# Two fp32 transformer blocks on one core: the first mixer's linear-attention steps are placed in other attention units, and x is normed by half blocks

## The chip, the cores and the metric

The kernel runs on one core of a Trainium2 chip. The metric is the device time in microseconds (us), the median of several runs. A profiled execution is one more run, recorded by the hardware profiler. TensorE is called PE here (PEld its weight loads), VectorE DVE, ScalarE ACT, GpSimd POOL, and SyncE SP, which here only issues transfers. Each engine works through its own list of instructions in order; semaphores hold an instruction until what it needs is there.

## The reference

Two blocks follow each other on x of 512 tokens by 1024 channels, all in fp32. Only the first mixer is touched by the change:

```python
u = rmsnorm(x, norm_mix_pre)
proj = u @ w_in        # qa ka va ga za | qs ks vs
# gated linear attention, 4 heads, chunks of 64 tokens, forwards and backwards
la = log_sigmoid(z @ w_gate_up + b_gate) / 16      # z: 16 of the 32 za columns
b = cumsum(la within a chunk)
q_dec, k_intra, k_state = q * exp(b), k * exp(-b), k * exp(b_last - b)
# windowed attention, 8 heads of 64, blocks of 128 tokens, keys of the block and its neighbours
logits = q @ k.T * 0.125 + rel_bias                # plus one sink logit per head
p = softmax(logits); o_s = p @ v
h = x + rmsnorm(concat(o_a, o_s) @ w_out)          # then an MLP, then the second block
```

## The kernel before

A product in fp32 quality is made of three products of rounded halves: a value is split in an upper part (rounded, made by ACT with a copy: `w_hi`, `act_hi`) and a lower part (value minus upper, made by DVE: `w_lo`, `act_lo`). `mm3` on PE multiplies hi by hi, hi by lo and lo by hi (L805 to L807).

The first mixer reads w_in in chunks c = 0 to 9 of 256 columns through two slots (`raw`, `w_hi`, `w_lo`). SP loads a chunk into its slot of `raw` when the lower part of the chunk two before has been made (`lo_done`). Chunks 0 and 1 are the queries of the windowed attention, 2 its keys and values, 3 the columns za (`zz`, only 128 columns are multiplied), 4 and 5 `qa` and `ka`, 6 and 7 `va_tok`, 8 and 9 `ga`.

**Start.** PE spreads the gain of the norm over the partitions (L836, into `psT`, two banks). ACT takes each block's sum of squares and its root (`first_scale`, L1442 to L1447), DVE multiplies the block of 128 tokens of x with its scale and the gain (`first_normed`, L2100, into `un`), PE turns it (`turn_first`, L858), ACT writes the upper part (`first_turned`, L1460) and DVE the lower part (L2109). Chunks 0 and 1 (`project_queries`) are multiplied for token blocks 0 and 1 as soon as those are turned (half 0, four groups of 24 matmuls named by a half of K and a slot: (0,0), (0,1), (1,0), (1,1)); blocks 2 and 3 are turned in between, and half 1 follows.

**The order of the rest** is one list of steps (`mixer1_steps`), which every engine walks and of which it takes its share. After chunks 2 and 3 come 18 attention units k = 0 to 17 (`attention_unit(k, work)`). Unit k holds, in this order: the logits matmuls of attention step k (`qk`, L1071), the transposes of the probabilities of step k-1 (`transpose`, PE L1082; ACT then copies them to `pT`, L1564), the softmax of step k (DVE L1964 to L1971, then ACT's two exponentials, L1556), at every fourth unit a `spread` of the inverse sums by DVE (L1983), then `work`, then at every fourth unit `turn` (PE L1106, ACT copy L1568, and DVE's product L1994 at the end of the unit), and the product with the values of step k-1 (`pv`, L1096). `work` is half an output tile of a chunk (12 matmuls of 512 columns, or 24 of 256 for the values), ACT's upper part of the next chunk (`split_hi`, L1435) at k = 0, 4, 8, 12, 16, DVE's lower part (`split_lo`, L1808) at k = 1, 5, 9, 13, 17, and the steps of the linear attention. These come four times, i = 0 to 3 (direction i % 2, channel half i // 2):

- `gla_gate`: PE L1114 multiplies the gate, DVE L2002 adds the bias, ACT does three functions (L1575 to L1577);
- `gla_decay`: DVE does three operations, the running sum among them (L2008, L2014, L2020), ACT three exponentials (L1583, L1584, L1586);
- `gla_scaled`: POOL makes two scaled key tiles (L1351, L1353, L1356; two SBUF inputs each), DVE copies the decay and scales the query (L2027, L2031);
- `gla_keys`: PE turns one of the key tiles (L1120), ACT copies it (L1589).

In the kernel before, gate, decay and scaled of i stand at the end of units 4 to 15, three units for each i (gate of i = 0 in front of the work of unit 4), so that decay 0 and 3 and scaled 1 fall into units with a lower part; keys stand in units 8, 11, 14 and 17.

**Between chunks 2 and 3** the step `keys_values` does three things: ACT copies the keys to the other 64 partitions (L1546, L1547), PE turns the values v (L1057), and ACT copies those out (L1549). `split` of chunk 4 and the tile of chunk 3 follow it.

Of the kernel before, what the change touches and what calls it, by code (L numbers as in the profile page):

```python
# [8 lines left out]
ALU = mybir.AluOpType  # L9
# [5 lines left out]
NBLK = TOK // P  # L15
# [186 lines left out]
def block_kernel(nc, a, out):  # L202
    ctx = ExitStack()
    with ctx:
# [338 lines left out]

        def mixer1_steps():
            steps = first_steps(0)
            steps += [("keys_values", 0), ("split", 4), ("tile", 3, 1)]
            k = 0
            for c in (4, 5, 6, 7, 8):
                for m, half in enumerate(half_tiles(c)[:2 if c == 8 else 4]):
                    work = [half]  # L550
                    if m == 0 and c < 9:
                        work.insert(0, ("split_hi", c + 1))
                    if m == 1 and c < 9:
                        work.insert(0, ("split_lo", c + 1))
                    if k >= 8 and k % 3 == 2:
                        work.insert(0, ("gla_keys", (k - 8) // 3))
                    if 4 <= k <= 15:
                        gla = (("gla_gate", "gla_decay", "gla_scaled")[(k - 4) % 3], (k - 4) // 3)
                        work.insert(0 if k == 4 else len(work), gla)
                    steps += attention_unit(k, work)  # L560
                    k += 1
            rest = half_tiles(8)[2:] + half_tiles(9)
            steps += [("gla_dS", 0), rest[0], rest[1], ("wsplit", N_O0, 1), ("gla_dS", 1), rest[2], rest[3],
                      ("gla_A", 0), rest[4], ("gla_A", 1), rest[5], ("attention_halves", 0),
                      ("gla_out", 0), ("gla_out", 1), ("gla_sum", 0), ("gla_sum", 1)]
            return steps
# [235 lines left out]
        def _(pe):  # L802
# [9 lines left out]
            def project_queries():  # L812

                for half in range(2):
                    cols = slice(HALF * half, HALF * half + HALF)
                    pe.wait_ge(act_lo_done, 4 * half + 4)
                    for kh, s in ((0, 0), (0, 1), (1, 0), (1, 1)) if half == 0 else ((0, 0), (1, 0), (0, 1), (1, 1)):
                        if half == 0:
                            pe.wait_ge(lo_done if kh else first_lo, s + 1)
                        for j in range(2):  # L820
                            for k in range(4 * kh, 4 * kh + 4):
                                last = mm3(acc[:, 2 * s + j, cols], *w_tiles(s, k, j),
                                           act_hi[:, k, cols], act_lo[:, k, cols], k == 0, k == KT - 1)
                            if half and kh:
                                last.then_inc(tile_done[j], 1)
                        if half == 0 and (kh, s) == (0, 0):
                            turn_tables()
                        if half == 0 and (kh, s) == (0, 1):
                            turn_first(2)
                    if half == 0:  # L830
                        turn_first(3)

            pe.wait_ge(const_in, 16)
            pe.wait_ge(gain1_in, 16)
            for g in range(2):
                last = pe.matmul(psT[:, g, :], ones[0:1, :], gain_row[:, 512 * g:512 * g + 512], start=True, stop=True)  # L836
            last.then_inc(gain1_ps, 1)

            def turn_tables():

# [6 lines left out]

            def turn_first(b):

                pe.wait_ge(un1_done, b + 1)  # L850
                if b >= 2:
                    pe.wait_ge(act_lo_done, 2 * (b - (1 if b == 3 else 2)) + 2)
                    if b == 2:
                        pe.wait_ge(vec_done, 1)
                        pe.wait_ge(relf_sb, 1)
                for g in range(2):
                    for k in range(4):
                        last = pe.transpose(first_bank(b, g)[:, k * P:(k + 1) * P],  # L858
                                            un1[:, b, (4 * g + k) * P:(4 * g + k + 1) * P], ident[:, :])
# [179 lines left out]
            def mixer_step_pe(layer, step, at):  # L1039
# [8 lines left out]
                elif what == "pair":  # L1048
                    project_queries()
                    last_in_bank.update({0: 0, 1: 1})  # L1050
                elif what == "keys_values":
                    if layer == 0:
                        pe.wait_ge(evac_done, 6)
                    else:
# [353 lines left out]
        def _(act):  # L1408
# [107 lines left out]
            def boundary_blocks(s, following):  # L1516
# [14 lines left out]
                    hi(N_AB, 0)  # L1531
                hi_turned(s, NBLK - 1)

            def mixer_step_act(layer, step):
                what, i = step[0], step[1]
                k = 16 * layer + i
# [1 line left out]
                    split(i)  # L1538
                elif what in ("wsplit", "upper"):
                    hi(i, step[2])  # L1540
                elif what == "keys_values":
                    if layer == 0:
                        act.wait_ge(evac_done, 6)
                    else:
                        act.wait_ge(evD_done, evacs_before(TILE_AT[N_KV, 0], "D") + 1)
                    act.activation(KX[layer][64:128, :], KH[layer][0:64, :], ACT.Copy).then_inc(kx_done, 1)  # L1546
                    act.activation(KX[layer][0:64, :], KH[layer][64:128, :], ACT.Copy).then_inc(kx_done, 1)  # L1547
                    act.wait_ge(vT_done, layer + 1)
                    act.activation(VTOK[layer][:, :, :], ps7[:, :].rearrange("p (b n) -> p b n", b=NBLK), ACT.Copy)\  # L1549
                       .then_inc(vtok_done, 1)  # L1550
                elif what == "softmax":
                    w = len(window(layer, i // 4)[0]) * P + 1
                    act.wait_ge(negmax_done, k + 1)
# [71 lines left out]
            first_scale(0)  # L1625
            first_scale(1)
            first_upper(0, 0)
            first_upper(0, 1)
            first_turned(0)
            first_turned(1)  # L1630
            first_scale(2)
            first_upper(1, 0)
# [166 lines left out]
        def _(dve):  # L1799
# [295 lines left out]
            def first_normed(b):  # L2095

                dve.wait_ge(rs1_done, b + 1)
                if b == 0:
                    dve.wait_ge(gain1_ps, 1)
                dve.scalar_tensor_tensor(out=un1[:, b, :], in0=x_tok[:, b, :], scalar=st1[:, b, 1:2],  # L2100
                                         in1=psT[:, :, :].rearrange("p g n -> p (g n)"), op0=ALU.mult, op1=ALU.mult)\
                   .then_inc(un1_done, 1)

            def first_lo_turned(b):

# [248 lines left out]
```

## Time and profile before

| | |
|---|---|
| runs | 1011.2, 1007.82, 1011.0 us, median 1011.0 |
| profiled execution | 1009.43 us, of it span 1007.6 us |
| PE busy | 980.5 us (97%) |
| DVE, ACT, POOL busy | 561.1, 397.4, 55.9 us |
| PE busy from 64 to 162 us (attention units) | 90.03 of 98 us |
| first matmul of the first product | at 16.31 us |

Start and duration are in us from the start of the span. A row in brackets says how long the engine had stood idle before the instruction and who ended it. PE is busy nearly throughout; where it stands is what the time could give.

### The profile page before, as it was taken

To read this page: it belongs to the slowest core of one execution; us is meant where nothing else is said; L and a number is where in the kernel's file an instruction comes from. 1 tells how busy PE (TensorE), PEld (TensorE's weight loads), DVE (VectorE), ACT (ScalarE), POOL (GpSimd) and SP (SyncE) were. 2 spreads that over 40 slices of the span, in tenths; PEclk is the share of its full clock that TensorE was granted. 3 is DMA by queue.
4 is the path that set the end of the run, shared out by engine and by line. 5 is a ranking of instruction groups with operands and counts; after the bars stand their busy time and mean duration, and the time that the engine had idled before them with its cause. 6 is when DMAs were issued, how large, how long until landed. Compare 5 with 4: busy or idle time off the path is not lost.

```text
span 1007.6 us, 12804 instructions
## 1 busy us (share of the span) xinstructions
PE 980.5 (97%) x5280; PEld 782.7 (78%) x5280; DVE 561.1 (56%) x721; ACT 397.4 (39%) x646; POOL 55.9 (6%) x49
## 2 busy tenths in 40 slices
PE   6999999999999999999999999999999999999997
PEld 4876777878888888888888888877778877667786
DVE  3356777657541244344234375356755568889953
ACT  5144563276432243134214354434564620222541
POOL 4000112000000000000000000003000100100300
PEclk9999999999999999999999999999999999999999
DMA  6942002232233322233222223422041556556112
GB/s 197 148 137 59 20 24 85 85 126 89 96 121 114 126 84 84 84 108 137 90 83 84 84 84 96 167 84 84 1 155 42 194 164 155 133 150 191 43 73 83
DMA packets 63361, 104.83 MB, mean 104 GB/s; under 512 B 3974, under 2 KB 27399, under 8 KB 63176
## 3 DMA queue, kind: packets, MB, share of 16 engines
q1 hardware_dynamic: 62968, 103.77, 32.9%
q8 instruction: 42, 0.69, 0.3%
q10 hardware_dynamic: 336, 0.25, 0.1%
q14 instruction: 15, 0.12, 0.0%
HBM read 99.43 MB, written 4.58 MB: 103 GB/s over the span
## 4 chain that ended last, share of the span: by engine, by line
PE 85%; DVE 9%; ACT 2%; issue 2%; DMA 1%; SPq 0%; DVEq 0%
PE acc L805 25%; PE acc L806 24%; PE acc L807 24%; PE psT L1082 2%; PE acc L1071 1%; PE psT L971 1%; PE ps L1096 1%; DVE wlr L1848 1%; DVE psT L2241 1%; PE psT L950 1%; DMA raw<-in_w_in_dram 1%; PE ps L971 1%; DVE sm L1970 1%; DVE rt L1875 1%; DVE stat L2256 0%
## 5 line engine op out<-in xcount | busy, mean ns | idle before, releaser
L805 PE MATMUL acc<-act_hi,wh 128*128 128x512 f32 x464 | 183.9, 396 | 0.3 <-DVE wlr L1848 0.3
L1848 DVE TENSOR_TENSOR wlr<-wl,wh 128x2048 fp32r<-128x2048 f32 (+1 forms) x66 | 145.2, 2204 | 64.7 <-ACT wh L1472 64.7
L807 PE MATMUL acc<-act_hi,wlr 128*128 128x512 f32 x464 | 181.1, 390 | 0.0
L806 PE MATMUL acc<-act_lo,wh 128*128 128x512 f32 x464 | 180.9, 390 | 0.0
L1472 ACT ACTIVATE wh<-wl 128x2048 fp32r<-128x2048 f32 (+1 forms) x68 | 124.3, 1832 | 60.0 <-DMA wl<-in_w_up_dram 34.2
L805 PE MATMUL acc<-wh,act_hi 128*128 128x512 f32 (+1 forms) x352 | 133.7, 380 | 0.6 <-DVE act_lo L1892 0.6
L807 PE MATMUL acc<-wh,act_lo 128*128 128x512 f32 (+1 forms) x352 | 130.6, 371 | 0.0
L806 PE MATMUL acc<-wlr,act_hi 128*128 128x512 f32 (+1 forms) x352 | 130.4, 371 | 0.0
L805 PEld LDWEIGHTS acc<-act_hi,wh 128*128 128x128 f32 x464 | 87.2, 188 | 22.9 <-issue 4.2
L807 PEld LDWEIGHTS acc<-act_hi,wlr 128*128 128x128 f32 x464 | 87.1, 188 | 18.6
L806 PE MATMUL acc<-wlr,hid_hi 128*128 128x512 f32 x256 | 100.9, 394 | 0.0
L806 PEld LDWEIGHTS acc<-act_lo,wh 128*128 128x128 f32 x464 | 87.3, 188 | 17.1
L805 PE MATMUL acc<-wh,hid_hi 128*128 128x512 f32 x256 | 100.6, 393 | 0.0
L807 PE MATMUL acc<-wh,hid_lo 128*128 128x512 f32 x256 | 99.5, 389 | 0.0
L805 PEld LDWEIGHTS acc<-wh,act_hi 128*128 128x128 f32 x352 | 66.5, 189 | 13.1 <-issue 1.6
L806 PEld LDWEIGHTS acc<-wlr,act_hi 128*128 128x128 f32 x352 | 66.5, 189 | 11.3 <-issue 0.7
L807 PEld LDWEIGHTS acc<-wh,act_lo 128*128 128x128 f32 x352 | 66.3, 188 | 11.4
L805 PE MATMUL acc<-act_hi,w_hi 128*128 128x512 f32 (+1 forms) x152 | 55.2, 363 | 4.0 <-DVE act_lo L2109 3.7
L1655 ACT ACTIVATE zr<-acc 128x512 f32<-128x512 f32 x32 | 19.2, 599 | 99.7 <-PE acc L807 99.7
L805 PEld LDWEIGHTS acc<-wh,hid_hi 128*128 128x128 f32 x256 | 48.1, 188 | 11.1
L807 PEld LDWEIGHTS acc<-wh,hid_lo 128*128 128x128 f32 x256 | 48.1, 188 | 10.6
L806 PEld LDWEIGHTS acc<-wlr,hid_hi 128*128 128x128 f32 x256 | 48.3, 189 | 9.5
(238 smaller groups left out, 1378.0 us busy)
## 6 DMA issues: line engine op xcount, KB each, us to landing
wl<-in_w_up_dram SPq DMA_DIRECT2D x16, 1024.0 KB, 6.4
wl<-in_w_down_dram SPq DMA_DIRECT2D x16, 1024.0 KB, 6.3
wl<-in_c_w_in_dram SPq DMA_DIRECT2D x20, 512.0 KB, 4.9
raw<-in_w_in_dram SPq DMA_DIRECT2D x18, 512.0 KB, 5.2
shifted<-glu_dram SPq DMA_DIRECT2D x32, 262.0 KB, 4.7
wl<-in_a_w_in_dram SPq DMA_DIRECT2D x8, 1024.0 KB, 6.2
wl<-in_w_out_dram SPq DMA_DIRECT2D x4, 1024.0 KB, 6.3
wl<-in_ab_w_out_dram SPq DMA_DIRECT2D x4, 1024.0 KB, 7.5
```

The source lines that it names most:

```text
L805: pe.matmul(dst, hi, x_hi, start=first, stop=False)
L806: pe.matmul(dst, hi, x_lo, start=False, stop=False)
L807: return pe.matmul(dst, lo, x_hi, start=False, stop=last)
L950: last = pe.transpose(psT[:, g, (k % 4) * P:(k % 4 + 1) * P], un[:, b % 2, k * P:(k + 1) * P], ident[:, :])
L971: last = pe.matmul(xsum(t)[32 * c:32 * c + 32, :], tapw[:, t % 2, 4 * m + c, :], shifted[:, t % 2, c, 4 * m:4 * m + TOK], start=m == 0, st ...
L1071: last = pe.matmul(acc[:, 2 + j, 0:len(kbs) * P], QH[layer][h64, hp, n * P:(n + 1) * P], keys[h64, kbs[0] * P:(kbs[-1] + 1) * P], start=Tr ...
L1082: last = pe.transpose(psTf[:, (2 * b + j) * P:(2 * b + j + 1) * P], LG[layer][:, i % 2, j, 1 + b * P:1 + (b + 1) * P], ident[:, :])
L1096: last = pe.matmul(ps6[64 * j:64 * j + 64, hp * P:(hp + 1) * P], VTOK[layer][:, kb, 64 * g:64 * g + 64], PT[layer][:, (2 * b + j) * P:(2 * ...
L1472: act.activation(wh[slot][:, kk, cols], wl[slot][:, kk, cols], ACT.Copy).then_inc(whi_done, 1)
L1655: act.activation(zr[:, m % 2, :], acc[:, TILES[e][2], :], ACT.Relu).then_inc(zr_done, 1)
L1848: dve.tensor_tensor(wlr[slot][:, kk, cols], wl[slot][:, kk, cols], wh[slot][:, kk, cols].bitcast(F32), ALU.subtract).then_inc(wlo_done, 1)
L1875: dve.scalar_tensor_tensor(out=rt[:, b, :], in0=yg[:, b, :], scalar=ssq[:, s, 12 + b:13 + b], in1=rt[:, b, :], op0=ALU.mult, op1=ALU.add). ...
```

## The change

It has four parts.

1. `first_normed` is done by halves of 512 channels, each after its own half of the spread gain, and `turn_first` waits by halves. On ACT the upper part of block 0 (`first_turned(0)`) comes before the upper part of chunk 1's first half (`first_upper(0, 1)`).
2. `turn_first(3)` stands on PE between the groups (1,0) and (1,1) of half 0, not behind (1,1).
3. `keys_values` is cut in two: `keys` (ACT's two copies) stays; `values` (PE's transposes and ACT's copy) comes behind the tile of chunk 3.
4. Gate, decay, scaled and keys have other units: gates at the end of units 2, 6, 10, 14; decays in front of the work of units 3, 7, 11, 15; scaled in front of that of units 6, 8, 12, 16; keys in front of that of units 7, 10, 14, 17.

```diff
-            steps += [("keys_values", 0), ("split", 4), ("tile", 3, 1)]
+            steps += [("keys", 0), ("split", 4), ("tile", 3, 1), ("values", 0)]
+            gla_first = {3: [("gla_decay", 0)], 6: [("gla_scaled", 0)], 7: [("gla_keys", 0), ("gla_decay", 1)],
+                         8: [("gla_scaled", 1)], 10: [("gla_keys", 1)], 11: [("gla_decay", 2)], 12: [("gla_scaled", 2)],
+                         14: [("gla_keys", 2)], 15: [("gla_decay", 3)], 16: [("gla_scaled", 3)], 17: [("gla_keys", 3)]}
+            gla_last = {2: ("gla_gate", 0), 6: ("gla_gate", 1), 10: ("gla_gate", 2), 14: ("gla_gate", 3)}
...
-                    if k >= 8 and k % 3 == 2:
-                        work.insert(0, ("gla_keys", (k - 8) // 3))
-                    if 4 <= k <= 15:
-                        gla = (("gla_gate", "gla_decay", "gla_scaled")[(k - 4) % 3], (k - 4) // 3)
-                        work.insert(0 if k == 4 else len(work), gla)
+                    work = gla_first.get(k, []) + work
+                    if k in gla_last:
+                        work.append(gla_last[k])
...
-                        if half == 0 and (kh, s) == (0, 1):
-                            turn_first(2)
-                    if half == 0:
-                        turn_first(3)
+                        if half == 0 and (kh, s) in ((0, 1), (1, 0)):
+                            turn_first(2 + kh)
...
-                last = pe.matmul(psT[:, g, :], ones[0:1, :], gain_row[:, 512 * g:512 * g + 512], start=True, stop=True)
-            last.then_inc(gain1_ps, 1)
+                pe.matmul(psT[:, g, :], ones[0:1, :], gain_row[:, 512 * g:512 * g + 512], start=True, stop=True)\
+                  .then_inc(gain1_ps, 1)
...
-                pe.wait_ge(un1_done, b + 1)
...
+                    pe.wait_ge(un1_done, 2 * b + g + 1)
...
             first_upper(0, 0)
+            first_turned(0)
             first_upper(0, 1)
-            first_turned(0)
             first_turned(1)
...
-                dve.scalar_tensor_tensor(out=un1[:, b, :], in0=x_tok[:, b, :], scalar=st1[:, b, 1:2],
-                                         in1=psT[:, :, :].rearrange("p g n -> p (g n)"), op0=ALU.mult, op1=ALU.mult)\
-                   .then_inc(un1_done, 1)
+                for g in range(2):
+                    if b == 0:
+                        dve.wait_ge(gain1_ps, g + 1)
+                    cols = slice(512 * g, 512 * g + 512)
+                    dve.scalar_tensor_tensor(out=un1[:, b, cols], in0=x_tok[:, b, cols], scalar=st1[:, b, 1:2],
+                                             in1=psT[:, g, :], op0=ALU.mult, op1=ALU.mult).then_inc(un1_done, 1)
```

ACT around the keys and values of the windowed attention: the rows begin with chunk 3's upper part and end with the first softmax. Before:

```order
L1433 ACTIVATE w_hi<-raw 128x8x128
L1546 ACTIVATE k1x<-k_72 64x512
L1547 ACTIVATE k1x<-k_72 64x512
L1549 ACTIVATE v_tok<-ps 128x512
L1435 ACTIVATE w_hi<-raw 128x2048
L1556 ACTIVATE lg_76,sums_80<-lg_76,sm_78 128x257 x2
```

Now:

```order
L1433 ACTIVATE w_hi<-raw 128x8x128
L1554 ACTIVATE k1x<-k_72 64x512
L1555 ACTIVATE k1x<-k_72 64x512
L1435 ACTIVATE w_hi<-raw 128x2048
L1537 ACTIVATE v_tok<-ps 128x512
L1563 ACTIVATE lg_76,sums_80<-lg_76,sm_78 128x257 x2
```

The upper part of chunk 4 (L1435) has moved in front of the copy of the turned values; on PE the turning itself stands behind the 24 matmuls of chunk 3's tile instead of in front of them.

DVE in units 5 and 6: from the last row of softmax 5 to the scaled query of i = 0 (`sq` is the gate tile here, `sq_sum` the running sum). Before:

```order
L1971 TENSOR_SCALAR sm_78<-sm_78 128x2
L1808 TENSOR_TENSOR w_lo<-raw,w_hi 128x2048
L1818 COPY ka<-acc 128x512
L2008 SCALAR_TENSOR_TENSOR sq<-sq 128x512
L2014 SCALAR_TENSOR_TENSOR sq_sum<-restart,sq 128x512
L2020 TENSOR_TENSOR sq<-sq_sum 128x512
L1964 COPY lg_76<-sink_82 128x2
L1965 SCALAR_TENSOR_TENSOR lg_76<-acc,bias_70 128x2x384
L1970 TENSOR_REDUCE sm_78<-lg_76 128x2
L1971 TENSOR_SCALAR sm_78<-sm_78 128x2
L2027 COPY decay<-eb 128x8
L2031 SCALAR_TENSOR_TENSOR qdec_f<-qa,eb 128x512
```

Now:

```order
L1978 TENSOR_SCALAR sm_78<-sm_78 128x2
L1815 TENSOR_TENSOR w_lo<-raw,w_hi 128x2048
L1825 COPY ka<-acc 128x512
L1971 COPY lg_76<-sink_82 128x2
L1972 SCALAR_TENSOR_TENSOR lg_76<-acc,bias_70 128x2x384
L1977 TENSOR_REDUCE sm_78<-lg_76 128x2
L1978 TENSOR_SCALAR sm_78<-sm_78 128x2
L2034 COPY decay<-eb 128x8
L2038 SCALAR_TENSOR_TENSOR qdec_f<-qa,eb 128x512
L2009 TENSOR_SCALAR sq<-ps,vec 128x512
```

Decay 0 has left the place between the lower part and softmax 6, and gate 1 has come in behind the scaled query.

DVE in units 3 and 4, from softmax 3 on. Before:

```order
L1971 TENSOR_SCALAR sm_78<-sm_78 128x2
L1818 COPY qa<-acc 128x512
L1964 COPY lg_76<-sink_82 128x2
L1965 SCALAR_TENSOR_TENSOR lg_76<-acc,bias_70 128x2x384
L1970 TENSOR_REDUCE sm_78<-lg_76 128x2
L1971 TENSOR_SCALAR sm_78<-sm_78 128x2
L1979 RECIPROCAL rsum_81<-sums_80 128x8
L1983 COPY spread_79<-rsum_81 128x512
L2002 TENSOR_SCALAR sq<-ps,vec 128x512
L1994 TENSOR_TENSOR o_60<-ps,o_60 128x4x128
```

Now:

```order
L1978 TENSOR_SCALAR sm_78<-sm_78 128x2
L2015 SCALAR_TENSOR_TENSOR sq<-sq 128x512
L2021 SCALAR_TENSOR_TENSOR sq_sum<-restart,sq 128x512
L2027 TENSOR_TENSOR sq<-sq_sum 128x512
L1825 COPY qa<-acc 128x512
L1971 COPY lg_76<-sink_82 128x2
L1972 SCALAR_TENSOR_TENSOR lg_76<-acc,bias_70 128x2x384
L1977 TENSOR_REDUCE sm_78<-lg_76 128x2
L1978 TENSOR_SCALAR sm_78<-sm_78 128x2
L1986 RECIPROCAL rsum_81<-sums_80 128x8
L1990 COPY spread_79<-rsum_81 128x512
L2001 TENSOR_TENSOR o_60<-ps,o_60 128x4x128
```

Decay 0 now stands right behind softmax 3, ahead of the copy of `qa` and of softmax 4, and the gate's bias is no longer in unit 4.

## Rows read from the trace of the kernel before

**Rows 1.** The page's chain that ended last: shares of the span by engine

```profile
PE 85%; DVE 9%; ACT 2%; issue 2%; DMA 1%; SPq 0%; DVEq 0%
```

**Rows 2.** What PE waited for, 0 to 260 us: total, times, longest

```profile
PE psT L1082 <- ACT lg L1556: 4.1, 4, 1.4
PE acc L805 <- DVE act_lo L2109: 3.7, 2, 2.2
PE ps L1096 <- ACT pT L1564: 2.1, 1, 2.1
...
PE ps L1106 <- DVE spread L1983: 1.4, 1, 1.4
PE ps L1057 <- DVE v L1818: 0.8, 1, 0.8
```

**Rows 3.** Two stretches: PE, PEld, DVE, ACT, POOL busy; clock, DMA share, GB/s

```profile
64.00:162.00 98.00, 90.03 (x640) 68.38 (x638) 68.23 (x116) 55.78 (x116) 10.14 (x8) 1.00 0.15 44
...
205.00:586.00 381.00, 381.00 (x1696) 314.14 (x1695) 164.39 (x160) 137.44 (x178) 0.00 (x0) 1.00 0.28 100
```

**Rows 4.** Timeline of PE at the start: start, duration, instruction

```profile
5.25 3.75 PE L836 MATMUL psT<-gain_row,ident_ones 1*128 1x512 f32 x4 [5.25 <-DMA gain_row<-in_norm_mix_pre_dram]
...
16.31 0.58 PE L805 MATMUL acc<-act_hi,w_hi 128*128 128x256 f32 x1 [2.18 <-DVE act_lo L2109]
...
19.68 0.36 PE L805 MATMUL acc<-act_hi,w_hi 128*128 128x256 f32 x1
...
20.83 0.25 PE L843 MATMUL ps<-ident_ones,vec_rows 97*128 97x97 f32 x1
...
34.16 0.39 PE L805 MATMUL acc<-act_hi,w_hi 128*128 128x256 f32 x1 [1.57 <-DVE act_lo L2109]
```

**Rows 5.** Timelines of ACT and DVE at the start

```profile
12.20 1.06 ACT L1453 ACTIVATE w_hi<-raw 128x1024 fp32r<-128x1024 f32 x1 [1.39 <-DMA raw<-in_w_in_dram]
...
14.12 1.08 ACT L1460 ACTIVATE act_hi<-acc 128x512 fp32r<-128x512 f32 x2
...
9.12 2.47 DVE L2100 SCALAR_TENSOR_TENSOR un<-x_tok,st,psT 128x1024 f32<-128x1024 f32 x2 [9.12 <-PE psT L836]
...
14.97 1.28 DVE L2109 TENSOR_TENSOR act_lo<-acc,act_hi 128x512 fp32r<-128x512 f32 x2
```

**Rows 6.** Timelines of PE and ACT around chunks 3 and 4

```profile
64.65 0.47 PE L805 MATMUL acc<-act_hi,w_hi 128*128 128x512 f32 x1 [0.23 <-DVE zz L1818]
...
50.56 1.06 ACT L1433 ACTIVATE w_hi<-raw 128x1024 fp32r<-128x1024 f32 x1 [8.36 <-DMA raw<-in_w_in_dram]
...
59.40 1.92 ACT L1435 ACTIVATE w_hi<-raw 128x2048 fp32r<-128x2048 f32 x1
```

**Rows 7.** Timelines of PE, DVE and POOL in units 5 and 6

```profile
88.56 0.88 PE L1082 MATMUL psT<-ident_ones,lg 128*128 128x128 f32 x6
92.14 0.88 PE L1096 MATMUL ps<-pT,v_tok 128*64 128x128 f32 x12
...
99.96 0.88 PE L1096 MATMUL ps<-pT,v_tok 128*64 128x128 f32 x12 [2.06 <-ACT pT L1564]
...
95.56 0.68 DVE L2008 SCALAR_TENSOR_TENSOR sq<-sq 128x512 f32<-128x512 f32 x1
...
98.15 0.16 DVE L1964 COPY lg<-sink 128x2 f32<-128x2 f32 x1
...
100.20 1.19 DVE L1971 TENSOR_SCALAR sm<-sm 128x2 f32<-128x2 f32 x1
...
100.08 1.28 POOL L1353 TENSOR_TENSOR sq_sum<-ka,sq 128x512 f32<-128x512 f32 x1
```

**Rows 8.** Groups of 64 to 162 us by shape: busy us, mean ns

```profile
L1808 DVE TENSOR_TENSOR w_lo<-raw,w_hi 128x2048 fp32r<-128x2048 f32 x4 | 9.1, 2284 | 0.0
...
L1965 DVE SCALAR_TENSOR_TENSOR lg<-acc,bias 128x768 f32<-128x768 f32 x8 | 7.6, 950 | 0.0
...
L1556 ACT ACTIVATE lg<-lg,sm 128x385 f32<-128x385 f32 x16 | 9.7, 609 | 10.4 <-DVE sm L1971 10.4
```

More of the change, by code:

```diff
@@ L1050, in mixer_step_pe @@
                     last_in_bank.update({0: 0, 1: 1})
-                elif what == "keys_values":
+                elif what in ("keys_values", "values"):
                     if layer == 0:
@@ L1532, in boundary_blocks, with values_turned @@
                 hi_turned(s, NBLK - 1)
+            def values_turned(layer):
+                act.wait_ge(vT_done, layer + 1)
+                act.activation(VTOK[layer][:, :, :], ps7[:, :].rearrange("p (b n) -> p b n", b=NBLK), ACT.Copy)\
+                   .then_inc(vtok_done, 1)
             def mixer_step_act(layer, step):
@@ L1540, in mixer_step_act @@
                     hi(i, step[2])
-                elif what == "keys_values":
+                elif what == "values":
+                    values_turned(layer)
+                elif what in ("keys_values", "keys"):
                     if layer == 0:
@@ L1547, in mixer_step_act @@
                     act.activation(KX[layer][0:64, :], KH[layer][64:128, :], ACT.Copy).then_inc(kx_done, 1)
-                    act.wait_ge(vT_done, layer + 1)
-                    act.activation(VTOK[layer][:, :, :], ps7[:, :].rearrange("p (b n) -> p b n", b=NBLK), ACT.Copy)\
-                       .then_inc(vtok_done, 1)
+                    if what == "keys_values":
+                        values_turned(layer)
                 elif what == "softmax":
@@ L2097, in first_normed @@
                 dve.wait_ge(rs1_done, b + 1)
-                if b == 0:
-                    dve.wait_ge(gain1_ps, 1)
-                dve.scalar_tensor_tensor(out=un1[:, b, :], in0=x_tok[:, b, :], scalar=st1[:, b, 1:2],
-                                         in1=psT[:, :, :].rearrange("p g n -> p (g n)"), op0=ALU.mult, op1=ALU.mult)\
-                   .then_inc(un1_done, 1)
+                for g in range(2):
[4 more added lines that the diff above has]
+                                             in1=psT[:, g, :], op0=ALU.mult, op1=ALU.mult).then_inc(un1_done, 1)
             def first_lo_turned(b):
```

## Prediction

> **What bounds the kernel now.** I read the chain that ended last first: PE holds 85% of it, and ACT, DVE and transfers together 12% [rows 1]. So a microsecond counts only where PE stands. Next I read PE's own waits of the first 260 us, the part that the change touches [rows 2]. From the first product to the end of the attention units PE stands 12.1 us: 3.7 us in two waits for lower parts of x, 0.8 us for the values v, and in the units 4.1 us in four waits for ACT's exponentials, 2.1 us in one wait for the copy `pT`, 1.4 us for `spread`. The units' three entries are 7.6 us; the stretch from 64 to 162 us agrees (98 less 90.03 busy, with some issue time) [rows 3]. From 205 to 586 us PE is never idle and its loads are released by its own tiles, so what is won before is kept, and no more than these 12 us is to be had [rows 3].
>
> **Part 1, half blocks.** The first matmul of the product starts at 16.31, when DVE has ended the lower part of block 1 (14.97 + 1.28) [rows 4, 5]. Before it ACT worked off the upper part of chunk 1 at 12.20, which waits for its transfer, then block 0's two copies, and block 1's from 14.12 [rows 5]. Now block 0's copies (1.0 us) go into the 1.39 us in which ACT stood before 12.20. For that block 0 must be turned by about 11: the first half of the gain's four passes (5.25 to 9.0) [rows 4] is done near 7.2, DVE's first half block (0.65, a quarter of 2.47) near 7.9, its second follows the gain's end 9.0 and is done at 9.75 [rows 5]. PE turns from 9.0 on without the wait that it had, and ends block 0 near 11. The transfer sets 12.20 as before, so block 1's copies start at about 13.2, DVE's last lower part ends near 15.05, and PE starts at 15.1: 1.2 us. Below that nothing is gained beyond 0.7 if the copies of block 0 don't fit; above it the clock decides, see the rivals.
>
> **Part 2, block 3.** PE turns block 3, then stands 1.57 us before 34.16 for copy and lower part [rows 4]. With 24 matmuls of group (1,1) behind the turning (24 at the later pace: 9 in 1.15 us, so 3.1 us) the copy and the lower part, 1.57 + about 1 us of turning overlap, are hidden. Gain 1.55.
>
> **Part 3, keys and values.** PE no longer waits 0.8 us for v [rows 2]. Let T be the end of chunk 2's tiles (56.9 before). Before, chunk 4's tile starts at 64.65, T + 7.8 [rows 6]. Now PE needs T + 6.7 (tile 5.4, turning 0.6, logits 0.7), while ACT's key copies end at T + 2.0, the upper part of chunk 4 (1.92) at T + 3.95, DVE's lower part (2.28) at T + 6.25 [rows 6, 8] and the copy of `zz` behind it at T + 6.9. Chunk 4's tile waits for both: T + 7.0, gain 0.8, with 0.3 us of the wait moved to `zz`. The price if the cover is gone: chunk 3 lands at 50.5 [rows 6] and comes now after T only if T falls under 53; its upper part, lower part and the copy of k end at about 53.5 where nothing moves its transfer, and T becomes 56.9 less 2.75, or 54.1. That is 0.6 us of margin, and the transfer itself is released by DVE's table copy, which comes earlier too. So nothing is added.
>
> **Part 4, the units.** Why PE stands now: in unit 5 DVE does softmax 5, the lower part (2.28), `ka`, then decay 0 (95.56 to 98.15, 2.6 us) before softmax 6 [rows 7, 8]. ACT's three decay exponentials wait for the sum and stand in front of the copy `pT`, so pv waits 2.06 us at 99.96, and softmax 6 is late for the next transposes [rows 7]. Decay 3 repeats it in unit 14, scaled 1 in unit 9, and decay 2 in unit 11 delays the spread.
>
> Now I lay the units end to end by these durations: logits 0.85 (0.63 with two key blocks), transposes and pv 0.81 or 0.59, half a tile 2.75 (from 88.56 + 0.81 to 92.14) [rows 7], values 2.95, DVE's softmax 2.15 (two of 0.95 and two small ones), ACT's pair of exponentials 1.2 (two of 0.609) [rows 8], decay 2.6. A loop from logits to transposes must fit into one unit. The tightest places come out so:
> - Unit 6, transposes of step 5. From the end of pv 3: ACT ends the upper part of chunk 6 at +0.8, the `turn` copy at +1.3; DVE's product at +1.9, softmax 5 at +4.1; exponentials +5.3. PE: logits 0.85, transposes 0.81, half a tile 2.75, pv 0.81, logits 0.85, in all 6.1. Margin 0.8.
> - Unit 12, spread behind decay 2 and softmax 12: 0.4 of margin.
> - Steps 9, 13 and 15: 1.2 to 1.6, two of them with a lower part but no decay in front of them, or the decay behind the softmax.
> - pv behind the decay's three exponentials: 1.5 or more, since these now start early in the unit.
>
> No decay shares a unit with a lower part, and nothing waits twice. The 7.6 us go to near 0; for the misses of such a sum I leave 0.4.
>
> What speaks against it is POOL. At 100.20 DVE's negation (1.19 us, else 0.17) lies over POOL's key product of 100.08 to 101.36 and ends with it [rows 7]: 1.0 us lost. The scaled keys now start with the softmax of their unit, in units 6, 8 and 12, so the sink's copy or the negation will be held again. By my laying out it is 0.4 us in unit 6, up to 1.3 in unit 8, 1.0 in unit 12, and all of it inside the margins of 1.3, 2.6 and 2.0 of those transposes; but unit 8's may push the spread 0.35 past PE.
> The Trainium skill (SBUF — State Buffer, "SBUF: two separate sides") calls the port pair of DVE and GpSimd an exclusive lock that is held for a whole instruction, while the loser fully blocks. By that rule, the trace agrees: the stall ends with POOL's instruction, and eight products could hold DVE for up to 1.3 us each; the sum would change by the 0.35 us alone.
>
> **Sum.** 1.2 + 1.55 + 0.8 + 7.6 - 0.4 = 10.75 us. The profiled execution took 1009.4 with a span of 1007.6; less 10.75 it is 998.7. It lies 1.6 us under the median 1011.0 of the runs, within their spread of 3.4. I say 999.2. The bound from above is the 12 us of all waits plus 1.5 of clock, from below the sure parts.
>
> **Rivals.**
> - *The units keep half of their waits* (each softmax late by a held negation or a queue that I laid too tight): 3.8 us stay, 1003. Speaks for it: margins of 0.4 and 0.8 us are small. Against: waits that are missed so add tenths. Chance 0.17.
> - *The waits only move*: the 2.6 us of DVE's decay in front of `qa`, `ka` and softmax 4, 8, 12 take the place of those removed, and only parts 1 to 3 count: 1009.4 - 3.55 = 1005.9, 1007 by the median. DVE's busy 68 of 98 us speaks against it [rows 3]. Chance 0.08.
> - *The clock.* The first 15 matmuls take 3.37 us, 0.225 each (the half level, 1.2 GHz), those from 19.68 to 20.83 take 0.128 (2.4 GHz) [rows 4]. Before them PE had stood 2.18 us. PE now works from 5.25 to about 13 with no gap, so the rise may come before the product: 15 times 0.1, 1.5 us more, 997.7. Or the rise stays at 19.7 and half of part 1 is lost, 0.6. Chance of the early rise 0.1.
>  The Trainium skill (TensorE: Matmul & The Clock Gate, "What's actually happening") says that the default state is throttled and activity releases the throttle; by it the first matmuls would gain as in this rival.
> - *Slower.* One mechanism: the loop through DVE and ACT, not PE, is the bound of the units. Then each of the four decays costs its 2.6 us and each of the four pairs of key products 2.5: 20.4 in all against the 11.1 us won, so 1018. It decides from the point where the units have no margin; the loop of unit 6 above would have to be 0.8 us longer and all others 1.2 to 2.6. The two engines stand 30 and 42 of 98 us [rows 3], most of it within each unit. Chance 0.03.
>
> **Numbers.** Forecast 0.62 (997 to 1001), the others 0.17, 0.08, 0.10, 0.03. The likeliest time is 999.2; the range for 8 in 10 takes in the early clock and half of the units' waits: 996.5 to 1003.5. A measurement of this kernel tells some 0.5% (5 us) from no change. Faster by more than that: 0.62 + 0.17 + 0.10, less 0.02 for a stay near the edge, 0.87; within it 0.10; slower 0.03.
>
> **What would show it.** The first matmul of the product near 15.1, the restart of half 1 near 31.4 with no wait, chunk 4's tile near 61, pv 15 ended near 151 instead of 162; in PE's waits no entry over 0.5 us for exponentials, `pT` or spread. DVE's small copies or negations of about 1.2 us beside POOL in units 6, 8 and 12 without a wait of PE behind them. I am wrong if PE waits for exponentials in units 6, 8, 9 or 12, if chunk 3 comes after T, or if a stretch behind 205 us has a wait that it did not have.

## The result and the profile after

The changed kernel takes 997.93 us (median of 4 runs, 996.52 to 998.65); the kernel before, run beside it, 1009.88 (4 runs, 1007.82 to 1011.2). The ratio is 0.9882 with a 95% interval of 0.9858 to 0.9906: faster by 1.2%. 999.2 was forecast. The profiled execution took 998.65 us (span 996.9), against 1009.43 (span 1007.6) before: 10.7 us less of span. It was the slowest of the four runs of after; the other three have no trace.

PE's waits from 0 to 250 us, as in [rows 2]: total, times, longest.

```profile
PE psT L836 <- DMA ident_ones<-in_shapes_dram: 5.4, 1, 5.4
PE acc L807 <- DVE act_lo L2117: 1.7, 1, 1.7
PE ps L1114 <- ACT o L1596: 0.8, 1, 0.8
PE acc L807 <- DVE zz L1825: 0.5, 1, 0.5
```

The entries for exponentials (4.1), `pT` (2.1), `spread` (1.4) and the values (0.8) are gone, and one of two waits for a lower part. New are 0.8 us of the gate's matmuls; the wait for `zz` has grown from 0.2 to 0.5. A wait of 1.5 us for the normed block, ahead of block 0's turning, is gone too. The two stretches of [rows 3], moved to where the same work now lies:

```profile
60.00:151.00 91.00, 89.66 (x644) 68.64 (x641) 67.02 (x117) 56.69 (x117) 10.28 (x8) 1.00 0.15 47
...
194.00:575.00 381.00, 381.00 (x1695) 313.85 (x1695) 164.56 (x160) 137.62 (x178) 0.00 (x0) 1.00 0.28 100
```

PE stands 1.3 us where it stood 8, with nearly the same matmuls (644 and 640 rows); 381 us of the later stretch are as full as before, so what is won ahead of it stays won. PE at the start and at chunk 4 (start, duration, instruction), for [rows 4] and [rows 6]; the row at 21.40 is the second group of the product:

```profile
9.10 2.03 PE L858 MATMUL ps<-ident_ones,un 128*128 128x128 f32 x8
...
14.57 0.58 PE L807 MATMUL acc<-act_hi,w_hi 128*128 128x256 f32 x1 [1.74 <-DVE act_lo L2117]
...
19.64 0.41 PE L809 MATMUL acc<-act_hi,w_lo 128*128 128x256 f32 x1
19.86 0.36 PE L843 MATMUL ps<-ident_ones,vec_rows 97*128 97x97 f32 x1
20.15 1.32 PE L846 MATMUL ps<-hot,relw 33*8 33x512 f32 x2
21.40 0.39 PE L807 MATMUL acc<-act_hi,w_hi 128*128 128x256 f32 x1
...
61.50 0.47 PE L807 MATMUL acc<-act_hi,w_hi 128*128 128x512 f32 x1 [0.54 <-DVE zz L1825]
```

The same second group in the kernel before:

```profile
21.01 1.02 PE L846 MATMUL ps<-hot,relw 33*8 33x512 f32 x2
21.96 0.39 PE L805 MATMUL acc<-act_hi,w_hi 128*128 128x256 f32 x1
```

The product starts 1.74 us earlier, but all 24 matmuls of its first group now run at the half level (0.213 us apart), where 15 did before, and so do part of the small table matmuls behind them (L843, L846). The next group starts only 0.56 us earlier: the clock takes 1.18 us, 0.77 in the group and 0.41 in the tables. Half 1 starts near 31.9 with no wait, and chunk 4's tile 3.15 us earlier. The rows of pv 15 end at 151.24 (150.58 and 0.66) and before at 162.11 (161.45 and 0.66): 10.87 us earlier, so 7.72 come from the units.

ACT at the start, for [rows 5]: block 0's two copies lie ahead of chunk 1's upper part (L1453), as laid out. The second one is the first row here. The upper part follows it without a gap, though its transfer had landed near 11.4 (issued at 2.1, 9.3 us to landing): in this execution the copies held it by 0.25 us.

```profile
11.16 0.60 ACT L1460 ACTIVATE act_hi<-ps 128x512 fp32r<-128x512 f32 x1 [0.32 <-PE ps L858]
11.65 1.05 ACT L1453 ACTIVATE w_hi<-raw 128x1024 fp32r<-128x1024 f32 x1
12.60 1.08 ACT L1460 ACTIVATE act_hi<-acc 128x512 fp32r<-128x512 f32 x2
```

DVE, POOL and PE in units 6, 8 and 12, for [rows 7]:

```profile
93.66 0.69 DVE L1978 TENSOR_SCALAR sm<-sm 128x2 f32<-128x2 f32 x1
...
104.50 0.94 DVE L1978 TENSOR_SCALAR sm<-sm 128x2 f32<-128x2 f32 x1
...
105.58 0.43 DVE L1990 COPY spread<-rsum 128x512 f32<-128x512 f32 x1
...
128.35 1.31 DVE L1990 COPY spread<-rsum 128x512 f32<-128x512 f32 x1
...
93.03 1.29 POOL L1353 TENSOR_TENSOR sq_sum<-ka,sq 128x512 f32<-128x512 f32 x1
...
104.12 1.30 POOL L1356 TENSOR_TENSOR ka<-ka,sq 128x512 f32<-128x512 f32 x1
...
128.08 1.29 POOL L1353 TENSOR_TENSOR sq_sum<-ka,sq 128x512 f32<-128x512 f32 x1
...
106.07 0.65 PE L1106 MATMUL ps<-ident_ones,spread 128*128 128x128 f32 x4
...
129.99 0.60 PE L1106 MATMUL ps<-ident_ones,spread 128*128 128x128 f32 x4
```

Three small operations of DVE (0.17, 0.17 and 0.43 us where POOL rests) take 0.69, 0.94 and 1.31. The first two end within 0.03 us of the end of a key product of POOL, the third 0.29 us behind it. No wait of PE stands behind them: `spread` is done at 106.01 and 129.66, the turning that needs it starts at 106.07 and 129.99.

### The profile page after: what moved, and what is told of

Read it like the earlier page. It is cut to its first block, busy times and chain, and to the rows that moved or that the text cites. A ratio compares the mean times of both kernels' runs of the same rounds, so it can differ in the third digit from the quotient of the medians.

```text
span 996.9 us, 12808 instructions
## 1 busy us (share of the span) xinstructions
PE 980.5 (98%) x5280; PEld 782.9 (79%) x5280; DVE 559.6 (56%) x725; ACT 398.0 (40%) x646; POOL 56.3 (6%) x49
## 4 chain that ended last, share of the span: by engine, by line
PE 88%; DVE 8%; ACT 2%; issue 2%; DMA 0%; DVEq 0%
PE acc L807 25%; PE acc L808 25%; PE acc L809 25%; PE acc L1071 2%; PE ps L1096 2%; PE psT L1082 2%; PE psT L971 1%; DVE wlr L1855 1%; DVE psT L2249 1%; PE psT L950 1%; PE ps L971 1%; DVE rt L1882 1%; DVE stat L2264 1%; DVE ysum L2239 0%; DMA ident_ones<-in_shapes_dram 0%
## 5 line engine op out<-in xcount | busy, mean ns | idle before, releaser
L808 PEld LDWEIGHTS acc<-wlr,act_hi 128*128 128x128 f32 x352 | 66.4, 189 | 11.4 <-issue 0.7
L809 PEld LDWEIGHTS acc<-wh,hid_lo 128*128 128x128 f32 x256 | 48.1, 188 | 10.7
```

Source lines behind the costliest of these rows:

```text
L808: pe.matmul(dst, hi, x_lo, start=False, stop=False)
L809: return pe.matmul(dst, lo, x_hi, start=False, stop=last)
```

## Experiments

Times are medians; "the kernel before" was run beside each (medians 1009.0, 1008.9, 1009.1 in the three groups of runs). "After without" undoes one part. After itself was measured beside a median of 1009.9 for the kernel before, so its time and that of an experiment come from different groups: medians alone do not tell differences of under 1 us between the two. Where such a difference counts, the steadier measure is a stretch of the trace, as from the start of the product's second group to chunk 4's tile: 42.66 to 42.70 us in all five kernels that have neither part 2 nor part 3.

**Part 4 alone** (`units_only`) and **after without part 4** (`no_units`):

```diff
# the kernel before with:
+            gla_first = {3: [("gla_decay", 0)], 6: [("gla_scaled", 0)], ...}
+            gla_last = {2: ("gla_gate", 0), ...}
-                    if k >= 8 and k % 3 == 2: ...
-                    if 4 <= k <= 15: ...
+                    work = gla_first.get(k, []) + work
+                    if k in gla_last:
+                        work.append(gla_last[k])
```

> The kernel before with part 4 alone: gate, decay, scaled and keys in the new units. My theory (the waits of the units came from a decay or a scaled step in a unit that also has a lower part, and they are gone): the start and chunk 4's tile stand where they stood (16.3 and 64.65), pv 15 ends near 154.3 instead of 162.04, PE's waits in the units fall from 7.6 us to under 1, in all 7.7 us faster, a ratio near 0.9924. Rival (the parts need each other, the earlier start makes the room in the units): under 5 us faster. Rival (waits were paid by the clock or by chance between executions): pv 15 moves by less than 3 us.

Measured: 1000.91 us (999.48 to 1001.16), ratio 0.9917 (0.9902 to 0.9933).

> The changed kernel with part 4 undone (parts 1 to 3 alone). Theory: parts 1 to 3 are worth 3.15 us (chunk 4's tile at 61.5 instead of 64.65) and the units keep their 7.6 us of waits: ratio near 0.997 against the kernel before, pv 15 ended near 159. Rival (the earlier start lets the units' waits shrink too): more than 5 us faster.

Measured: 1005.85 us (1004.1 to 1007.45), 0.9966 (0.9953 to 0.998); all waits of the units are back (4.1, 2.1, 1.4). Part 4 is worth 8.1 us alone and 7.9 with the rest by the medians, 7.8 and 7.7 by the stretch from chunk 4's tile to pv 15: the parts add, and it is most of the gain.

**Part 1 alone** (`start_only`, half blocks and ACT's swap) and **after without part 1** (`no_start`); the edits are part 1's lines of the diff above.

> The kernel before with part 1 alone: x by half blocks and ACT's swap. Theory: the first matmul of the product comes at 14.6 instead of 16.3; if the clock rises as late as in the changed kernel (only after 20 us), the second group of matmuls starts 0.5 us earlier only and the whole gain is 0.5 us, ratio 0.9995; if it rises 3.4 us behind the first matmul as in the kernel before, the gain is 1.7 us. The wait of 1.57 us in front of half 1 stays in both cases, since block 3 is still turned behind all of half 0.

> The changed kernel with part 1 undone (parts 2 to 4). Theory: first product matmul at 16.1 to 16.3, all else kept: 0.6 to 1.8 us slower than the changed kernel (by how late the clock rises in it), about 999.5. Rival (parts 2 or 4 need the earlier start, as the turning of block 3 then comes before its block is normed): over 2.5 us slower, with a wait of PE before the transposes of block 3.

Measured: 1007.73 (1005.91 to 1008.74), 0.9985 (0.9975 to 0.9995); and 998.83 (996.75 to 999.37), 0.9892 (0.9876 to 0.9909), 0.9 more than after. Some 1 us, at the limit of what the runs tell. The traces are sharper. The transfer of chunk 1 lands at a time that differs from one execution to the next: with the old order ACT starts its upper part at the landing, at 11.15 (`turn3_only`) to 12.20 us (before). From the upper part's start to the first matmul of the product it is 4.11 to 4.12 us in every kernel with the old order (before 12.20 to 16.31; `units_only` 11.76 to 15.88; `no_start` 12.02 to 16.14) and 2.91 to 2.92 in every kernel with part 1 (after 11.65 to 14.57; `start_only` 11.63 to 14.55). Where ACT has its copies done before the landing, as in `start_only`, part 1 gives these 1.20 us. In after it had not, and 0.25 of them are lost: the old order would have put the product at 11.4 + 4.12 = 15.5, so some 1.0 of the 1.74 us is part 1, and some 0.75 is a transfer that happened to come earlier.

In `start_only` the first group has 15 slow matmuls, as before, and the second group starts 1.83 us earlier, with nothing lost to the clock; the wait ahead of half 1 stays (1.57). In `no_start` the stretch from the second group to chunk 4's tile is that of after (40.11 and 40.10 us): parts 2 and 3 do not need part 1.

**ACT's swap alone** (`swap_only`, in the kernel before):

```diff
             first_upper(0, 0)
+            first_turned(0)
             first_upper(0, 1)
-            first_turned(0)
```

> The kernel before with only ACT's order changed: block 0's two copies ahead of the upper part of chunk 1's first half; the norm stays in whole blocks. Theory of the prediction (the swap needs the half blocks, since block 0 must be turned by about 11): block 0 is turned at 12.4, ACT's two copies end near 13.0, the upper part of chunk 1 near 14.0, block 1's copies near 15.1 against 15.2 before, and the product starts at 16.1 to 16.3, nothing won (1008.8 to 1009). Rival: the swap alone wins what part 1 wins, the first matmul at 15.1 or earlier.

Measured: 1008.0 (1007.06 to 1010.24), 0.9986 (0.9975 to 0.9996).

```profile
9.06 1.06 ACT L1453 ACTIVATE w_hi<-raw 128x1024 fp32r<-128x1024 f32 x1 [0.88 <-DMA raw<-in_w_in_dram]
11.25 0.60 ACT L1460 ACTIVATE act_hi<-ps 128x512 fp32r<-128x512 f32 x1 [1.13 <-PE ps L858]
12.11 0.60 ACT L1460 ACTIVATE act_hi<-ps 128x512 fp32r<-128x512 f32 x1 [0.26 <-PE ps L858]
12.60 1.05 ACT L1453 ACTIVATE w_hi<-raw 128x1024 fp32r<-128x1024 f32 x1
...
15.51 0.38 PE L805 MATMUL acc<-act_hi,w_hi 128*128 128x256 f32 x1 [1.73 <-DVE act_lo L2109]
```

The second upper part of w starts at 12.60 behind the late copies. Its data was there near 11.5 (issued at 2.1, 9.4 us to landing), and the old order would have put the product at 15.6. The swap alone wins some 0.1 us; it needs the half blocks. The profiled execution (1007.06 us) is faster for two other causes: its transfer came 0.7 us earlier than that of before, and its 24 first matmuls are all 0.12 us apart (below). What makes up the 1 us of the medians is not shown; the other nine runs have no trace.

**Part 2 alone** (`turn3_only`, in the kernel before; the edit is part 2's lines of the diff):

> The kernel before with part 2 alone: block 3 is turned between the groups (1,0) and (1,1) of half 0. Theory: it pays by itself, as copy and lower part are hidden under 3.1 us of matmuls: no wait ahead of half 1, whose first matmul comes at 32.5 instead of 34.16, chunk 4's tile at 63.0, time 1007.3 (1.6 to 1.75 less). Rival: it pays only behind part 1, since with the later start DVE's first block sets when blocks 2 and 3 are normed and the turning of block 3 now waits in the middle of the half; then a wait of 1 us or more stands ahead of the turning of block 3 and the time is 1008.5 or more.

Measured: 1006.26 (1005.65 to 1009.28), 0.9973 (0.9961 to 0.9985). Half 1 starts at 31.53 without a wait. From the start of the second group, where the clock is at its full level in both, to chunk 4's tile it is 40.86 us against 42.69: part 2 gives 1.83 us by itself. The median is 2.8 us under that of before; what the rest is, the trace of one execution does not show.

**Decay 0 back at the end of unit 5** (`decay0_back`, in after):

```diff
-            gla_first = {3: [("gla_decay", 0)], 6: ...
+            gla_first = {6: ...
+                    if k == 5:
+                        work.append(("gla_decay", 0))
```

> The changed kernel with decay 0 alone moved from the front of unit 3 to the end of unit 5, which has a lower part (where it stood before). Theory (the collision in one unit is the cause): DVE does softmax 5, lower part, ka, decay 0 and only then softmax 6; pv 4 or the transposes of step 6 wait again, 2 to 3.5 us in all in units 5 to 7, nowhere else, 1000.5 in all. Rival (what counts is DVE's total or the gate's place): under 0.5 us of new wait.

Measured: 999.61 (999.08 to 1000.2), 0.9907 (0.9888 to 0.9926), 1.7 more than after. PE in units 6 and 7:

```profile
94.55 0.88 PE L1098 MATMUL ps<-pT,v_tok 128*64 128x128 f32 x12 [0.90 <-ACT pT L1573]
...
97.36 0.88 PE L1084 MATMUL psT<-ident_ones,lg 128*128 128x128 f32 x6 [1.09 <-ACT lg L1565]
```

One decay behind a lower part brings back both kinds of wait of [rows 7], the copy `pT` behind ACT's exponentials and the transposes behind a late softmax: 2.0 us for one misplaced step (the stretch to pv 15 is 2.07 us longer).

**The two waits that the change brought** (`better`, in after): keys 1 one unit earlier, chunk 4's upper part ahead of the copies of the keys.

```diff
-            steps += [("keys", 0), ("split", 4), ("tile", 3, 1), ("values", 0)]
+            steps += [("split", 4), ("keys", 0), ("tile", 3, 1), ("values", 0)]
-                         8: [("gla_scaled", 1)], 10: [("gla_keys", 1)], ...
+                         8: [("gla_scaled", 1)], 9: [("gla_keys", 1)], ...
```

> The changed kernel with two steps moved: keys 1 from unit 10 to unit 9, and the upper part of chunk 4 in front of the two key copies on ACT. Theory: the wait of 0.8 us before gate 2 in unit 10 was for ACT's copy of keys 1, which stands behind the exponentials of its own unit, and the 0.54 us before chunk 4's tile was for zz, whose copy stands on DVE behind the lower part of chunk 4: both go, 1.3 us faster than the changed kernel, about 996.6. Rival (another wait stands right behind each, as the transposes of step 9): under 0.5 us.

Measured: 996.99 (995.92 to 997.67), 0.9877 (0.9862 to 0.9891), 0.9 less than after, which the medians alone would not tell. The stretches do: from the second group to chunk 4's tile 39.51 us against 40.10, and from that tile to pv 15 0.55 us less, 1.1 in all of the 1.3 expected. All of PE's waits up to 250 us are now:

```profile
PE psT L836 <- DMA ident_ones<-in_shapes_dram: 5.0, 1, 5.0
PE acc L807 <- DVE act_lo L2117: 2.3, 1, 2.3
PE ps L1120 <- issue: 0.3, 1, 0.3
```

In after, the cause of the 0.8 us was this row of ACT, with the softmax of its unit ahead of it:

```profile
117.89 0.57 ACT L1596 ACTIVATE o<-ps 128x512 f32<-128x512 f32 x1
...
118.61 1.09 PE L1114 MATMUL ps<-zz,gate_w 32*128 32x512 f32 x2 [0.81 <-ACT o L1596]
```

In unit 10 the turned keys are copied out behind the two exponentials of step 10, and gate 2 needs the same PSUM bank at the end of the unit. In unit 9 the copy has a unit's time.

**Unused matmuls in PE's gap.** `fill_gap` is after with four matmuls of the identity, whose product nobody reads, behind the turning of block 1; `warm_early` has these and eight more ahead of the gain, on a tile that POOL clears first; `fill_before` has the four in the kernel before.

```diff
             turn_first(0)
             turn_first(1)
+            for _ in range(4):
+                pe.matmul(acc[:, 0, 0:P], ident[:, :], ident[:, :], start=True, stop=True)
```

> The changed kernel with work for PE that no result uses: 8 small matmuls on a zeroed tile before the gain and its constants have landed, and 4 behind the turning of block 1, where PE stands 1.7 to 2.1 us. If the clock follows PE's activity, PE reaches the high level before or soon after 5 us, the gain and the turning take half their time, and the 24 matmuls of the first group run at 0.12 us instead of 0.22: the first product matmul still comes near 14.4 (ACT and the transfer set it), its group ends 2.4 us sooner, tile of chunk 4 near 59.1, 2.4 us faster than the slowest start seen (chunk 4's tile at 61.5), 1 us than the fastest (60.07). Rival (the rise is a matter of chance in each execution, whatever PE does): slow matmuls at the start as before.

> The changed kernel with the 4 extra matmuls in the gap between the turning of block 1 and the product alone. Theory: PE is then busy without a gap from 5.3 us on and the rise comes before 17 us; the first group has under 12 slow matmuls. Rival (the start of PE's work, not the gap, sets it): 14 to 24 slow ones as in the kernels without it.

> The kernel before with only the four unused matmuls put behind the turning of block 1, where PE stands for 2.18 us. Theory that PE's standing ahead of the product is what has it start at the half level: no slow matmul among the first group, its 24 matmuls take 3 us instead of 4.5 (15 slow ones by 0.1), chunk 4's tile at 63.1 instead of 64.65, the rest unchanged, time 1007.4 (1.5 less). Rival: the clock rises at a fixed time near 19.6 whatever PE does before the product (as the last slow matmul of five of the eight kernels so far would have it): 15 slow matmuls, no change of the time beyond 0.1 us.

Measured: `warm_early` 997.48 (995.55 to 998.0), 0.9879 (0.9863 to 0.9895); `fill_gap` 995.88 (995.75 to 996.19), 0.9867 (0.9851 to 0.9884), 2.0 less than after; `fill_before` 1007.89 (1007.08 to 1010.0), 0.9991 (0.998 to 1.0002), not told from no change by its runs. `warm_early`, which also has the four, is only 0.5 us under after: its profiled run took 995.55 us, the other three 997.4 to 998.0. PE in `fill_gap`, with the four matmuls in the first row:

```profile
12.45 1.81 PE L865 MATMUL acc<-ident_ones 128*128 128x128 f32 x8
14.58 0.39 PE L807 MATMUL acc<-act_hi,w_hi 128*128 128x256 f32 x1 [0.32 <-DVE act_lo L2119]
14.80 0.28 PE L808 MATMUL acc<-act_lo,w_hi 128*128 128x256 f32 x1
14.92 0.28 PE L809 MATMUL acc<-act_hi,w_lo 128*128 128x256 f32 x1
```

The product starts where it did in after (14.57) and runs at the full level. Its second group starts at 18.68 instead of 21.40, 2.7 us earlier, which is the whole loss to the clock in the profiled execution of after (6.83 us from the product's start to the second group, here 4.10). The matmuls ahead of the gain in `warm_early` did nothing: the gain and block 0's turning still took as long. The four do not close the gap: PE still stood 0.32 us behind them in `fill_gap`, 1.24 in `best` and 1.59 in `fill_before`, without a slow matmul, where `turn3_only` stood 1.52 us without them and had 17. So it is what PE did before it stood, or chance, and not the length of the standing alone.

**All three finds together** (`best`: `better` with the four unused matmuls):

> The kernel after with the three edits found good so far together: the keys' step of i = 1 in unit 9, the upper part of chunk 4 ahead of the copies of the keys, and four unused matmuls behind the turning of block 1. If the two unit edits and the filling of PE's gap are independent of each other, their gains add: the product starts at 14.6 with no slow matmul, chunk 4's tile comes near 58.2, the chunk 8 and 9 stretch as in the kernel with the filling less another 1 to 1.4 us, so the end of the third keys' turning is at 147.4 to 147.9 and the time 994.6 to 995.2 us. Rival: the faster start brings a new wait (chunk 3's transfer comes after the tiles of chunk 2), which takes the unit edits' 1.3 us back; then chunk 4's tile is at 58.8 or later and the time is 995.9, that of the filling alone.

Measured: 995.0 us (994.42 to 995.16), 0.9854 (0.9837 to 0.9872). It is the fastest kernel, 2.9 us under after; the gains add (0.9 and 2.0 by the medians). Chunk 4's tile starts at 57.81 with no wait, and the turned keys of i = 3 come at 147.28 (162.36 before).

```profile
PE psT L836 <- DMA ident_ones<-in_shapes_dram: 5.1, 1, 5.1
PE acc L807 <- DVE act_lo L2119: 1.2, 1, 1.2
PE ps L1122 <- issue: 0.3, 1, 0.3
```

## Why the prediction held, by its own steps

**Part 1, forecast 1.2, is 1.20** where the copies of block 0 fit ahead of the transfer, and some 1.0 in after, where they end 0.25 late; the step named this loss (nothing beyond 0.7 if they don't fit) but took the transfer to land at 12.20 as before. And the rival in which the clock stays low till 19.7 took 1.18 us, more than all of part 1, and not the 0.6 that I gave it: 0.77 in the first group, and 0.41 in the tables behind it, which I had left out. By chance the transfer came some 0.75 us earlier and made up for over half of that.

**Part 2, forecast 1.55, is 1.83.** The term held the wait alone. But PE's next instruction overlaps the end of the one before it, and ahead of a wait this overlap is lost too. Block 2's turning, with work ready behind it, is followed after 0.79 us (24.94 to 25.73); block 3's in the kernel before runs to its end, 1.03 us, before the wait begins. That is 0.24 of the 0.26 us beyond the wait of 1.57.

**Part 3, forecast 0.8, is 0.76.** From the second group to chunk 4's tile it is 40.86 us with part 2 alone and 40.10 to 40.12 in all six kernels with parts 2 and 3 and keys first. The wait moved to `zz` as the step said, 0.54 instead of 0.3. In `better`, which makes chunk 4's upper part first, it is gone, worth another 0.6. Chunk 3 did not become late: its upper part starts at 50.66, T is 54.3 (54.1 forecast), and PE does not wait for it.

**Part 4, forecast 7.6 less 0.4 for misses, is 7.72.** No wait for exponentials, `pT` or `spread` is left. The miss was real, and twice as large: 0.8 us at gate 2, where keys 1 (ACT's copy) stands behind the softmax of unit 10. I had laid out DVE's and ACT's loops up to the transposes and pv, but not the gate's matmuls, which need the bank of the turned keys. What made up for it: the six waits of the units held 7.6 us, and the stretch is 7.72 shorter with 0.8 of new wait in it, so 0.9 more went than waits show. Some 0.2 of it has no wait: gate 0 no longer stands between the transposes and the tile of unit 4, where the transposes took 0.59 us to the next start (82.09 to 82.68), now 0.41 (80.01 to 80.42). Some 0.5 is the overlap lost ahead of a wait, as in part 2: 0.06 us where logits stand before it (92.94 to their end 93.85, where an undisturbed unit has 0.85 to the next start), 0.2 in unit 12. The rest I can't place. It is no fixed price for each wait: the two waits of `decay0_back` hold 1.99 us and cost 2.07.

**The margins** were laid too wide. Unit 6's was 0.8 by my sum: in the trace the exponentials of step 5 end at 90.15 and the transposes start at 90.43, 0.28 us. ACT's upper part of chunk 6 ends 0.96 us, and the exponentials 5.7 us, behind pv 3; I had 0.8 and 5.3. Unit 8's spread, which I feared 0.35 past PE, was 0.06 ahead. `decay0_back` shows what lies beyond the margin: 2 us for 2.6 us of DVE.

**POOL's holds** came where the sum had them: 0.5 us in unit 6 (forecast 0.4), 0.8 in unit 8 (up to 1.3), 0.9 in unit 12 (1.0), none with a wait behind it.

**The rivals.** "Units keep half their waits" and "waits only move" fell with the waits; `no_units` and `units_only` show the 8 us directly. "Slower" fell with them. The clock's early rise did not happen in after. With the four unused matmuls it did, and gave 2.0 us by the medians and 2.7 in the traces where the rival had 1.5, since 24 and not 15 matmuls are slow in the profiled execution of after.

So the sum of 10.75 against a measured 10.87 at pv 15 is closer than its terms, and that is luck: by the measured ones it is 1.0 + 1.83 + 0.76 + 7.72, less 1.18 for the clock, plus 0.75 from the transfer, 10.88. The median of after, 997.93, is 1.3 us under the 999.2 that I said; a first group with fewer slow matmuls in its other runs would do that, but they have no trace.

## What to carry to other kernels

Where in-order engines share a stage, no unit should hold two of the long steps that stand ahead of a softmax; lay the loop out by each engine's durations, and include every matmul that reuses a bank which another engine must first empty. Judge a change at the start from a landing transfer to the matmul that it releases, since the landing itself moves by a microsecond between executions (11.15 to 12.20 us here). Compare stretches of the trace that begin behind the slow matmuls; here they agree to 0.04 us between kernels, where the times of the kernel before alone spread by 4.8. If PE stands shortly before a long product, look at the pace of its first matmuls; a few unused matmuls in the gap gave 2.0 us in two pairs here, but only 0.5 in a third.

## What the runs showed of the hardware

**The level of TensorE's clock at the start.** Without the unused matmuls, the profiled executions of ten kernels had 0 to 24 slow matmuls in the first group (0.213 us apart, the 1.2 GHz level; else 0.12, 2.4 GHz). In `before`, after, `start_only`, `no_units`, `turn3_only` and `better` the product started slow, though the granted clock of these stretches is shown as 1.00: there the pace of equal matmuls is the surer sign. In `units_only`, `no_start` and `decay0_back` it started fast and fell back soon after, and there the granted clock shows it. In all ten PE turned two blocks and then stood 1.5 to 2.5 us. `units_only`, PE's rows and then the busy times as in [rows 3] of two stretches:

```profile
16.22 0.28 PE L809 MATMUL acc<-act_hi,w_lo 128*128 128x256 f32 x1
16.34 0.28 PE L807 MATMUL acc<-act_hi,w_hi 128*128 128x256 f32 x1
16.46 0.38 PE L808 MATMUL acc<-act_lo,w_hi 128*128 128x256 f32 x1
16.63 0.41 PE L809 MATMUL acc<-act_hi,w_lo 128*128 128x256 f32 x1
...
15.88:16.45 0.57, 0.57 (x4) 0.57 (x5) 0.00 (x0) 0.00 (x0) 0.00 (x0) 1.00 0.13 50
16.50:19.80 3.30, 3.30 (x17) 3.30 (x17) 0.00 (x0) 3.18 (x6) 0.51 (x1) 0.50 0.04 13
```

The level came back between 17.9 us (`start_only`) and later than 20.1 (after, by its row at 20.15). In the profiled executions of the four kernels with the four unused matmuls no matmul of the product was slow. But `swap_only`, with 1.73 us of standing, had none either: without them the low level is likely, not certain, and what decides it in a single execution stays open, with one profile of each kernel. The two pairs `fill_gap` with after and `best` with `better` both differ by 2.0 us; `warm_early` with after by 0.5; the pair in the kernel before by 1.2, which its interval does not tell from nothing. The Trainium skill (TensorE: Matmul & The Clock Gate, "What's actually happening") has the clock start throttled and activity release it; the rows above agree, and add that it can fall again within the first microseconds of the product.

**The same in the units.** The level also fell there, behind the wait of 2.1 us for `pT` that part 4 removes, in two of the six kernels that still have it (`turn3_only` and `fill_before`). The logits behind it took 1.69 us instead of 0.91. `turn3_only`:

```profile
97.23 1.19 PE L1094 MATMUL ps<-pT,v_tok 128*64 128x128 f32 x12 [2.09 <-ACT pT L1562]
...
98.00:99.00 1.00, 1.00 (x6) 0.52 (x6) 1.00 (x3) 0.32 (x1) 0.63 (x1) 0.50 0.00 0
101.00:102.00 1.00, 1.00 (x7) 0.86 (x6) 0.96 (x2) 0.57 (x1) 0.00 (x0) 0.97 0.00 0
```

It cost less than the slow matmuls, since the next wait, 1.1 us for the exponentials, is gone in these two: from chunk 4's tile to pv 15 they take 0.46 us more than before. So a wait of PE can cost more than its time, and not in every execution. In the kernels with part 4 there was no such fall in any trace.
